# 24 of 128 pieces of an expert table multiplied 512 columns at a time, with the two halves of each result added on the way out of PSUM

## The reference, cut to what matters

```python
def peer_ffn(xn, w_q, keys1, keys2, u_tab, v_tab):
    q = (xt @ w_q).reshape(T, PEER_HEADS, PEER_QDIM)
    s1 = einsum('thd,hkd->thk', q[..., :half], keys1)
    s2 = einsum('thd,hkd->thk', q[..., half:], keys2)
    v1, i1 = top_k(s1, 16); v2, i2 = top_k(s2, 16)
    ...                      # sums of all pairs, top_k again, softmax
    u = take(u_tab, ec, axis=0)
    act = einsum('td,thkd->thk', xc, u)
    hact = gelu(act) * gc
    return einsum('thk,thkd->td', hact, take(v_tab, ec, axis=0))
```

## Time and profile before

| | value |
|---|---|
| median of three runs | 2843.96 us |
| the profiled execution's own time | 2845.44 us |
| its span, first to last instruction | 2843.6 us |
| PE busy | 2808.2 us (99%) |
| DVE busy | 1950.2 us (69%) |
| ACT busy | 1632.7 us (57%) |
| POOL busy | 338.8 us (12%) |
| chain that ended last | PE 90%, DVE 6%, ACT 2% |

### The profile page before, as it was taken

How to read it: one execution, slowest core, us unless ns; L and a number is a source line. 1 busy time by engine, 2 the same in 40 slices (tenths; PEclk the granted TensorE clock), 3 DMA queues, 4 the chain that set the end, 5 groups by cost and what they waited for, 6 DMA issues and landing times.

```text
span 2843.6 us, 44337 instructions
## 1 busy us (share of the span) xinstructions
PE 2808.2 (99%) x17826; PEld 2539.4 (89%) x17826; DVE 1950.2 (69%) x3363; ACT 1632.7 (57%) x2792; POOL 338.8 (12%) x310
## 2 busy tenths in 40 slices
PE   8999999999999999999999999999999999999999
PEld 7888888888988888899999999999888889999997
DVE  6656765776676676768865998776555566766775
ACT  5554654755665564566645445776544455655663
POOL 0000000000010002000001445895000000000000
PEclk9999999999999999999999999999999999999999
DMA  6655566466435555345265554334555564536454
GB/s 215 200 166 168 168 199 226 137 196 221 149 123 193 201 197 176 111 155 186 74 202 173 189 178 163 124 132 162 193 193 194 193 240 127 171 107 215 139 197 147
DMA packets 304539, 490.32 MB, mean 172 GB/s; under 512 B 10880, under 2 KB 236544, under 8 KB 295632
## 3 DMA queue, kind: packets, MB, share of 16 engines
q1 hardware_dynamic: 303200, 480.09, 51.1%
q0 software_dynamic: 1136, 7.41, 0.7%
HBM read 485.37 MB, written 2.10 MB: 171 GB/s over the span
## 4 chain that ended last, share of the span: by engine, by line
PE 90%; DVE 6%; ACT 2%; DMA 1%; issue 1%; POOL 0%; DVEq 0%; POOLq 0%; SPq 0%; ACTq 0%
PE ps L634 30%; PE ps L566 11%; PE ps L562 11%; PE ps L563 11%; PE ps L717 11%; PE ps L716 6%; PE ps L583 3%; PE ps L1151 2%; DVE halves L1397 2%; PE ps L1186 1%; DVE R L1397 1%; PE ps L515 1%; DVE AR L2304 1%; PE ps L874 0%; PE ps L1205 0%
## 5 line engine op out<-in xcount | busy, mean ns | idle before, releaser
L2668 ACT ACTIVATE halves<-raw 128x1024 fp32r<-128x1024 f32 (+2 forms) x834 | 870.3, 1052 | 673.7 <-PE ps L634 322.6
L1397 DVE TENSOR_TENSOR halves<-raw,halves 128x1024 fp32r<-128x1024 f32 (+1 forms) x798 | 955.0, 1218 | 219.1 <-ACT halves L2668 216.2
L562 PE MATMUL ps<-XX,halves 128*128 128x256 f32 (+1 forms) x2360 | 586.7, 286 | 0.0
L563 PE MATMUL ps<-XX,halves 128*128 128x256 f32 (+1 forms) x2360 | 578.3, 283 | 0.0
L634 PE MATMUL ps<-halves,XX 128*128 128x512 f32 x2160 | 501.0, 392 | 2.0 <-DVE XX L1412 1.1
L634 PEld LDWEIGHTS ps<-halves,XX 128*128 128x128 f32 x2160 | 405.6, 188 | 88.0 <-issue 2.7
L562 PEld LDWEIGHTS ps<-XX,halves 128*128 128x128 f32 (+1 forms) x2360 | 451.5, 191 | 0.8
L563 PEld LDWEIGHTS ps<-XX,halves 128*128 128x128 f32 (+1 forms) x2360 | 452.0, 192 | 0.3
L566 PE MATMUL ps<-XX,halves 128*128 128x256 f32 (+1 forms) x2360 | 331.5, 283 | 0.7 <-DVE halves L1397 0.7
L717 PE MATMUL ps<-XX,halves 128*128 128x512 f32 x1264 | 319.1, 394 | 2.8 <-DVE XX L1435 2.8
L634 PE MATMUL ps<-halves,R 128*128 128x512 f32 x1404 | 321.2, 389 | 0.0
(11 more groups left out here) (367 smaller groups left out, 3546.6 us busy)
## 6 DMA issues: line engine op xcount, KB each, us to landing
raw<-in_w_ffn_in SPq DMA_DIRECT2D x88, 1024.0 KB, 5.1
raw<-in_w_in SPq DMA_DIRECT2D x74, 1024.0 KB, 5.2
raw<-in_uT SPq DMA_DIRECT2D x64, 1024.0 KB, 4.8
raw<-in_peer_v SPq DMA_DIRECT2D x64, 1024.0 KB, 4.9
raw<-in_w_ffn_out SPq DMA_DIRECT2D x44, 1024.0 KB, 4.8
raw<-in_w_up SPq DMA_DIRECT2D x24, 1024.0 KB, 5.7
raw<-in_mlstm_w_in SPq DMA_DIRECT2D x12, 1024.0 KB, 5.4
raw<-in_w_down SPq DMA_DIRECT2D x12, 1024.0 KB, 4.9
```

The lines of the kernel that those rows point to most:

```text
L562: mm(o[:, ts], hi[:, q, 0:M], xh[:, k0 + q, ts], start=first and q == 0, stop=False)
L563: mm(o[:, ts], hi[:, q, 0:M], xl[:, k0 + q, ts], start=False, stop=False)
L1397: te.tensor_tensor(lo, src, hi.bitcast(F32), ALU.subtract).then_inc(k.lo_made, 1)
L2668: act(hi, src, ACT.Copy).then_inc(k.hi_made, 1)
```

## The change

A constant `WIDE = 24` is added. Pieces 0 to 23 of the first expert table go through `wide` and take one whole bank each, so that the four banks hold four pieces and not eight. At its odd position ACT copies the second half of each of the two new results into SBUF (two instructions of 128 x 256), and then applies gelu, SBUF to SBUF, to the pair before, for which it waits for DVE. At its even position DVE adds the first half of each result to that copy (two instructions of 128 x 256, one input in SBUF and one in PSUM), and it is this that frees the bank. The other 104 pieces are as before.

```diff
+WIDE = 24
...
+    def beside(self, n):
+
+        return self.ar(60 * 256 + n % 4 * 256, 256)
+
...
-        for n in range(128):
+        for n in range(WIDE):
+            wide(("pr.u", n), main, rx)
+        for n in range(WIDE, 128):
             if n % 2 == 0:
                 b = main.take(pe, ("pr.u", n))
...
 (DVE)   def taken(f):
             t = weighed_before(f) * 4
+            for n in range(f, f + 2 if f < WIDE else f):
+                m = k.beside(n)
+                v.wait_ge(*s["beside"].need(("pr.u", n)))
+                te.tensor_tensor(m, m, ps[:, main.of(("pr.u", n)), 0:256], ALU.add).then_inc(*main.done(("pr.u", n)))
...
 (ACT)   def taken(f):
+            if f < WIDE:
+                for n in (f, f + 1):
+                    a.wait_ge(*full["pr.u", n])
+                    if n >= 4:
+                        a.wait_ge(*s["act"].need(("pr.h", n - n % 2 - 4)))
+                    act(k.beside(n), ps[:, main.of(("pr.u", n)), 256:512], ACT.Copy).then_inc(*s["beside"].mark(("pr.u", n)))
+            if 2 <= f < WIDE + 2:
+                for n in (f - 2, f - 1):
+                    a.wait_ge(*main.gone(("pr.u", n)))
+                m = k.ar(60 * 256 + (f - 2) % 4 * 256, 2, 256)
+                act(hidden[:, f - 2:f, :], m, ACT.Gelu).then_inc(*s["act"].mark(("pr.h", f - 2)))
+            if f < WIDE:
+                return
             t = weighed_before(f) * 4
```

## The result

The changed kernel takes 2859.03 us (median of five runs, 2854.88 to 2859.79) against 2843.96 (2840.80 to 2845.59): ratio 1.0052, 95% interval 1.0041 to 1.0062, slower by 15 us. The forecast was 2864, range 2845 to 2871, slower.

What follows compares the result with a forecast made beforehand. PE was taken as the bound, DVE close behind. Terms of 13.4, 1.5 and 5.5 us sum to 20.4; on the median 2843.96, 1.5 below the profiled execution's 2845.44, that gives 2864 us, range 2845 to 2871.

Steps and rivals of the forecast that it cites:

- The matmuls: Pieces 0 to 23: sixteen matmuls replace 24, a piece takes 2.80 us instead of 2.88, so PE gains 1.9 us.
- DVE's loop: Wide pieces: with the adds DVE needs 6.2 us a pair where PE wants 5.6; its reserve lasts four pairs.
- The lock: From the `lo` of piece 14, DVE's `lo` waits for POOL's to end in every pair: 8.1 us a pair.
- Term 1: Piece 24 starts at 1622.9 instead of 1609.5: +13.4 us, with the 1.9 us matmul gain already in it.
- The case named for it: Among the wide pieces, the two close cases go to DVE and not POOL: 2 to 4 us less.
- Term 2: Behind piece 24, a late `lo` and long selection instructions near piece 28 hold PE: +1.5 us, bounds 0 and 4.
- Term 3: DVE stays late up to piece 50 and PE pays between pieces 50 and 72: +5.5 us, bounds 1 and 8.
- The rival of 5 us more: Wide pieces: POOL's `lo` blocks DVE's new adds too, reserve gone two to three pairs earlier; some 5 us more, upper bound.
- Rival A: Wide pieces: DVE's loop fits within 5.6 us, the adds are hidden and 1.9 us are gained: 2842 us; chance 10%.
- B: Wide pieces: DVE sets the pace but its `lo` gets ahead of POOL's each time, loop 6.2 us: 2847 us; chance 17%.
- C: DVE is caught behind POOL, but lateness dissolves up to 1700 or some turns are won: 2850 to 2856 us; chance 9%.
- D, the clock: Wide pieces: PE's clock drops to 1.2 GHz, 3.1 us more a pair for up to four pairs: 2877 us; chance 4%.

Runs made afterwards that it cites:

- POOL's short `lo`: The changed kernel, but POOL makes only the first of eight blocks of each `lo` of an odd piece below 32; 2846.23 us, ratio 1.0011.

## Why the prediction was right, point by point

- The matmuls, -1.9 us: measured -2.04 and -2.05 where nothing else is in the way. Right.
- DVE's loop 6.2 us against 5.6, the 2.5 us in hand gone after four pairs: DVE's adds came every 6.2 us (once 5.9) up to 1572.11. PE began piece 12 late by 0.26 us (the row of its matmuls at 1572.27 lasts 2.26 and not 2.00 us), and its first long wait for an add is at piece 14. Right.
- The lock with 8.1 us a pair from piece 14: 8.14 and 8.05 us between the adds of 1572.11, 1580.25 and 1588.30. Right, also in where it begins; the third turn was not locked (5.88 to the add at 1594.18).
- Term 1, +13.4 us at piece 24. Counted from the key products piece 24 started 76.37 us later before (1609.34) and 87.18 after (1618.89), which is +10.8. The case named for it had come in: of the two close turns, those of pieces 18 and 24, the first went to DVE (later that of piece 26 too). The six pairs took 1618.42 - 1572.11 = 46.3 us and not 48.6; that is 2.3 of the 2.6 us. By its own terms the sum had 0.3 too much as well: 1549.2 + 4 x 6.2 is 1574.0, not 1574.3.
- Term 2, +1.5: 0. PE waited for nothing between 1619 and 1713. This term was too large, though within its bounds (0 to 4).
- Term 3, +5.5: 15.4 - 10.8 = 4.6. DVE's `lo` stayed behind POOL's end up to piece 50, and PE paid at piece 56.

The first matmul of piece 24, before and after, for term 1:

```profile
1609.34 0.28 PE L562 MATMUL ps<-XX,halves 128*128 128x256 f32 x1
...
1618.89 0.39 PE L567 MATMUL ps<-XX,halves 128*128 128x256 f32 x1 [0.56 <-DVE AR L2362]
```

Timeline rows of the changed kernel for term 3: a `lo` of DVE behind POOL's, and PE's tail matmuls of pieces 55, 56 and 57.

```profile
1643.86 2.41 POOL L1299 TENSOR_TENSOR halves<-raw,halves 128x1024 fp32r<-128x1024 f32 x1 [3.35 <-ACT halves L2679]
...
1645.53 1.82 DVE L1404 TENSOR_TENSOR halves<-raw,halves 128x1024 fp32r<-128x1024 f32 x1
...
1710.19 1.12 PE L571 MATMUL ps<-XX,halves 128*128 128x256 f32 x8
1716.45 1.60 PE L571 MATMUL ps<-XX,halves 128*128 128x256 f32 x8 [3.22 <-DVE halves L1404]
1720.92 1.12 PE L571 MATMUL ps<-XX,halves 128*128 128x256 f32 x8
```

Two pieces took 10.73 us instead of 5.76: 3.4 for the wait, and 1.6 for a lower clock behind it.

- The adds and POOL: the Trainium skill, SBUF — State Buffer, section "Who interferes with whom", says that an instruction of DVE with at most one input in SBUF, outside the 2-port modes, does not contend with GpSimd. The 0.42 us beside POOL's `lo` in the version where POOL makes all of them agree, which before could only be bounded. The rival of 5 us more fell.
- Rival A fell: DVE's loop did not fit. B was seen in single turns, and whole with POOL's short `lo`, where piece 24 started 77.8 us behind the key products, 1.4 later than before (2 forecast). C was part of what happened. D, the clock, came in twice among the wide pieces, at no price, since DVE's loop was longer than even the slowed pair, and once at piece 56.

The sum, 20.4, was above the 15.4 measured: 2.6 in term 1, 1.5 in term 2, 0.9 in term 3. All three erred to the same side, so no two errors cancelled; but one turn won or lost is worth 2.2 us, and the turn of piece 18 was a tie to the hundredth, which no sum of this kind can tell. What stays open: the five timed runs of the changed kernel fall into two groups, near 2855 and near 2859.5. Turns that go one way or the other, or the clock behind a wait, could do that, but only one of the runs has a trace, so the split of the 15.4 us holds for the slower group.

## What to carry to other kernels

Price an added instruction against the slack of its engine's loop, not against its share of busy time; and when the loop has become the longer one, follow what starts the neighbours, because a wait can put two engines that never met into the same moment in every turn. DVE and POOL instructions that both read two inputs from SBUF are such neighbours: 0.6 us of lateness a pair became 2.5 us, and reordering, not removing, work took half of the stage's loss back. Where two engines share a job piece by piece, giving all of it to the one with time to spare can cost nothing and end the meeting.

## What the runs showed of the hardware

Two starts within the same hundredth of a us: DVE's `lo` at 1590.81 took 1.23, POOL's 3.49. At 1574.94, 0.32 after POOL, DVE's took 3.16. At 1620.93 they tied again, and DVE was first again (1.22 and 3.50). A tie in the record doesn't say who is served first, though; with POOL's short `lo` (up to 31) one went the other way, DVE's `lo` taking 1.53 us:

```profile
1608.73 0.46 POOL L1301 TENSOR_TENSOR halves<-raw,halves 128x128 fp32r<-128x128 f32 x1 [5.76 <-ACT halves L2681]
1608.73 1.53 DVE L1406 TENSOR_TENSOR halves<-raw,halves 128x1024 fp32r<-128x1024 f32 x1
```

TensorE's clock fell behind waits of 2 to 3 us, but not behind each. Windows of the changed kernel: stretch, length, busy us and instructions of PE, PEld, DVE, ACT, POOL, clock, DMA.

```profile
1572.30:1580.80 8.50, 6.19 (x35) 4.96 (x34) 8.09 (x24) 3.57 (x6) 2.40 (x1) 0.98 0.54 176
1580.80:1584.90 4.10, 4.08 (x15) 3.42 (x16) 3.89 (x12) 1.58 (x2) 2.15 (x1) 0.62 0.36 150
1584.90:1594.30 9.40, 8.63 (x51) 7.39 (x49) 8.82 (x32) 4.63 (x7) 3.73 (x2) 1.00 0.34 112
1602.80:1607.00 4.20, 4.11 (x22) 3.58 (x23) 4.00 (x12) 2.55 (x4) 2.17 (x1) 1.00 0.36 150
1716.40:1721.00 4.60, 4.55 (x25) 4.55 (x26) 4.57 (x6) 1.06 (x1) 0.00 (x0) 0.63 0.71 242
```

After a wait of 2.31 us the clock was at 0.62 on average over 4.1 us, that is mostly at the level of 1.2 GHz, and then back at 2.4. After another wait of 2.32 us (at 1602.89) it was 1.00. After the wait of 3.22 it was 0.63 over 4.6 us, 1.6 us of time. The same wait of 3.22 us in the version with eight banks was followed by matmuls at full pace (eight in 1.22 us instead of 1.60), so behind a wait of either length the clock sometimes fell and sometimes didn't.
